# Two blocks on one core: modulation quarters in two banks with the index key behind them, and x turned chunk by chunk with the norms' roots behind the products

## The reference, cut to what matters

```python
def _hybrid_layer(x, c, w_ada, b_ada, g_norm, w_in, ...):
    mod = jax.nn.silu(c) @ w_ada + b_ada
    shift, scale, gate = jnp.split(mod, 3, axis=-1)
    h = _rms_norm(x, g_norm) * (1.0 + scale[:, None, :]) + shift[:, None, :]
    proj = h @ w_in
    qa, ka, va, za, q_idx, k_idx, w_idx, qb, kb, vb, zb = jnp.split(proj, COL_SPLITS, axis=-1)
    k_idx = _rms_norm(k_idx, k_norm_idx)
    ...
    return x + gate[:, None, :] * y

def second_block(x, positions, attn_norm_g, w_in, ...):
    h = rms_norm(x, attn_norm_g[l])        # norm 2
    proj = h @ w_in[l]
    shifted = token_shift(proj[..., :RWKV_SHIFT_DIM], rwkv_mu[l])
    ...
    x = x + y @ w_out[l]
    h = rms_norm(x, ffn_norm_g[l])         # norm 3
    gate = conv1d(h @ w_gate) + conv_b
    x = x + (silu(gate) * (h @ w_up)) @ w_down
    return rms_norm(x, final_norm_g)
```

## Time and profile before

| | |
|---|---|
| median of 3 runs | 1993.59 us |
| profiled execution, its own time | 1993.05 us |
| its span (first to last instruction) | 1991.3 us |
| mean granted TensorE clock | 0.981 |
| PE / POOL / DVE / ACT busy | 95% / 67% / 46% / 41% |
| moved by DMA | 352.6 MB, mean 177 GB/s |

### The profile page before, as it was taken

One profiled execution on the slowest core, in us unless ns is written; L12 is line 12 of the kernel. 1 busy time (PEld: TensorE's weight loads), 2 busy tenths in 40 slices (PEclk: granted clock), 3 DMA queues, 4 the chain that ended last, 5 costly groups with the idle time before them and its releaser, 6 DMA issues.

```text
span 1991.3 us, 32274 instructions
## 1 busy us (share of the span) xinstructions
PE 1892.2 (95%) x12975; PEld 1582.5 (79%) x12975; DVE 906.2 (46%) x1122; ACT 809.2 (41%) x1095; POOL 1325.3 (67%) x683
## 2 busy tenths in 40 slices
PE   5889999999989899998999999999999999999997
PEld 2668878888657798887789877888888888888886
DVE  1004647560351324565644361654455555733223
ACT  3224444444444454333422444434334343433333
POOL 2448878888239489962543496798888888844442
PEclk8899999999999999999999999999999999999999
DMA  9984545555765356543100145455555555555553
GB/s 328 363 306 164 176 168 175 189 187 190 283 223 180 112 163 212 191 147 127 46 25 4 48 167 176 162 190 189 181 181 187 190 190 180 182 196 197 194 190 127
DMA packets 174433, 352.60 MB, mean 177 GB/s; under 512 B 6735, under 2 KB 19421, under 8 KB 171773
## 3 DMA queue, kind: packets, MB, share of 16 engines
q1 hardware_dynamic: 173437, 346.94, 52.4%
q10 hardware_dynamic: 896, 4.20, 0.6%
HBM read 349.02 MB, written 2.10 MB: 176 GB/s over the span
## 4 chain that ended last, share of the span: by engine, by line
PE 59%; POOL 20%; issue 18%; DVE 2%; ACT 1%; POOLq 0%; DVEq 0%; ACTq 0%
PE bank L919 21%; POOL WL L547 19%; PE bank L921 10%; PE bank L873 6%; PE bank L874 6%; PE bank L875 6%; PE bank L1265 5%; PE bank L1185 1%; PE bank L1195 1%; PE bank L1228 1%; PE bank L395 0%; PE bank L1154 0%; POOL HX L840 0%; POOLq L546 0%; POOL arena L814 0%
## 5 line engine op out<-in xcount | busy, mean ns | idle before, releaser
L547 POOL TENSOR_TENSOR WL<-WR,WH 128x1024 fp32r<-128x1024 f32 (+2 forms) x516 | 1229.4, 2393 | 487.1 <-ACT WH L1478 485.6
L1478 ACT ACTIVATE WH<-WR 128x1024 fp32r<-128x1024 f32 (+2 forms) x560 | 577.4, 1037 | 813.3 <-PE bank L875 450.3
L919 PE MATMUL bank<-HX,WH 128*128 128x512 f32 x1840 | 649.6, 398 | 6.9 <-POOL WL L547 5.2
L921 PE MATMUL bank<-HX,WL 128*128 128x256 f32 x1840 | 515.4, 280 | 0.0
L919 PEld LDWEIGHTS bank<-HX,WH 128*128 128x128 f32 x1840 | 345.6, 188 | 92.5 <-issue 5.9
L873 PE MATMUL bank<-WH,HX 128*128 128x512 f32 (+2 forms) x864 | 339.1, 393 | 12.3 <-POOL WL L547 7.3
L921 PEld LDWEIGHTS bank<-HX,WL 128*128 128x128 f32 x1840 | 347.2, 189 | 0.0
L875 PE MATMUL bank<-WH,HX 128*128 128x512 f32 (+2 forms) x864 | 331.5, 384 | 0.0
L874 PE MATMUL bank<-WL,HX 128*128 128x512 f32 (+2 forms) x864 | 331.3, 383 | 0.0
L873 PEld LDWEIGHTS bank<-WH,HX 128*128 128x128 f32 x864 | 163.0, 189 | 50.9 <-issue 14.0
L874 PEld LDWEIGHTS bank<-WL,HX 128*128 128x128 f32 x864 | 163.2, 189 | 31.1 <-issue 1.9
(11 more groups left out here) (295 smaller groups left out, 1957.9 us busy)
## 6 DMA issues: line engine op xcount, KB each, us to landing
WR<-in_w_in SPq DMA_DIRECT2D x96, 1024.0 KB, 5.0
WR<-in_ffn_w_gate SPq DMA_DIRECT2D x44, 1024.0 KB, 5.1
WR<-in_ffn_w_up SPq DMA_DIRECT2D x44, 1024.0 KB, 5.1
WR<-in_ffn_w_down SPq DMA_DIRECT2D x44, 1024.0 KB, 5.1
arena<-in_w_ada SPq DMA_DIRECT2D x64, 512.0 KB, 9.4
WR<-in_w_out SPq DMA_DIRECT2D x32, 1024.0 KB, 5.1
WR<-in_w_ada SPq DMA_DIRECT2D x16, 1024.0 KB, 5.1
WR<-in_w_in SPq DMA_DIRECT2D x12, 768.0 KB, 4.3
```

The costliest lines, as they stand in the source:

```text
L547: eng.tensor_tensor(half(WL, n % NSLOT, *w), half(WR, n % NSLOT, *w), half(WH, nth(n) % 2, *w), ALU.subtract).then_inc(ready, 1)
L919: pe.matmul(bank[:, :].rearrange("p (h n) -> p h n", h=2), wh[:, k, o], HX[:, :, kk, :], start=kk == 0, stop=False, skip_group_check=True)
L921: last = pe.matmul(bank[:, 0:L], wl[:, k, o], HX[:, 0, kk, :], start=False, stop=kk == KT - 1, skip_group_check=True)
L1478: act.activation(half(WH, nth(n) % 2, *w), half(WR, n % NSLOT, *w), ACT.Copy).then_inc(hi_ready, 1)
```

## The change

Three things are edited.

**Start.** Even quarters of the modulation go to BANK 0 and odd ones to BANK 1, so `mod_piece` waits for `mod_ready` from the third quarter on only. A quarter has three projection pieces. The index key is one piece of 16 row tiles by 128 columns (`n_kw`) behind the last quarter. SP's order is spaced anew, and ACT puts the first `high` of a quarter ahead of the row copy. PE turns the key inside chunk j = 1 (`key_turn`), and turns back the spread key inside chunk 2 (`key_spread`); ACT's share of it (`take_key`, `take_spread`) stands between `high(n + 2)` and `high(n + 3)`.

**Norms 2 and 3.** X is turned unscaled: groups 0 to 5 inside the output chunks of the next column chunk, groups 6 and 7 inside the first chunk that uses them. They go to buffers of their own, HX2 and HX3. The products are those of unnormed x. rstd comes in behind: ACT multiplies the c chunks as it takes them; for the rest PE spreads rstd over the partitions (`row_of`, ones × diag), DVE copies that row (`row_to`) and multiplies each product by it (`by_token`): one for wag, 6 in rkv, 22 in gate and up.

**Places.** Banks of output chunks, wag and c chunks are allotted anew, as are RAWF, CV, UPS, AH, AL and the gate row.

```diff
+        n_kw = n_in + 3 * PIECES
+        n_br = n_kw + 1 - PIECES
...
-            ada_quarter(0, 4, 8)
+            ada_quarter(0, 4, 7)
             for q in range(4):
                 in_piece(q, 0)
+                ada_quarter(q, 7, 8)
+                if q < 3:
+                    ada_quarter(q + 1, 0, 2)
                 in_piece(q, 1)
                 if q < 3:
-                    ada_quarter(q + 1, 0, 3)
+                    ada_quarter(q + 1, 2, 4)
                 in_piece(q, 2)
                 if q < 3:
-                    ada_quarter(q + 1, 3, 5)
-                in_piece(q, 3)
-                if q < 3:
-                    ada_quarter(q + 1, 5, 8)
+                    ada_quarter(q + 1, 4, 7)
+            load(n_kw, w_in[:, KW_COL:KW_COL + P].rearrange("(k p) n -> p k n", p=P), P, KT)
...
                 i = n % 8
                 pe.wait_ge(ada_in[n % 4], 32 * (n // 4 + 1))
-                if i == 0 and n >= 8:
-                    pe.wait_ge(mod_ready, n // 8)
+                if i == 0 and n >= 16:
+                    pe.wait_ge(mod_ready, n // 8 - 1)
                 for g in range(4):
                     o = slice(32 * g, 32 * g + 32)
-                    last = pe.matmul(BANK[0][o, :], CA[:, 2 * i + g // 2, :], ada_w[n % 4][:, g * CH:(g + 1) * CH],
+                    last = pe.matmul(BANK[n // 8 % 2][o, :], CA[:, 2 * i + g // 2, :], ada_w[n % 4][:, g * CH:(g + 1) * CH],
                                      start=i == 0, stop=i == 7)
                 last.then_inc(ada_done, 1)
...
-                for i, (token, first, width) in enumerate(((False, 1, P), (False, 4, CH), (False, 6, CH), (True, 2, CH))):
+                for i, (token, first) in enumerate(((False, 4), (False, 6), (True, 2))):
                     if q < 3:
...
-                    if q == 3 and i == 1:
-                        pe.wait_ge(kiT_taken, 1)
+                    piece(n_in + 3 * q + i, q, token, first, CH)
+            pe.wait_ge(act_took, 2)
+            piece(n_kw, 0, False, 4, P, KT)
...
+            def key_turn(kk):
+                if kk == 2:
+                    pe.wait_ge(kiT_taken, 1)
+                    pe.wait_ge(act_took, 4)
+                    for t in range(TT):
...
+                    last.then_inc(ki_ready, 1)
+            def key_spread(kk):
...
                         for t in range(TT):
-                            last = pe.transpose(BANK[0][:, t * P:t * P + P], KIT[:, t * P:(t + 1) * P], ident[:])
...
+                    last.then_inc(kixT_ready, 1)
...
-                    if b == 0 and j == 1:
...
+            def turn_x(g, base, updated):
+                pe.wait_ge(x_updated, updated + 2 * (g // 2 + 1))
+                to_feature(X, g, 4, base)
...
+            def row_of(bank, q):
+                pe.wait_ge(xn_ready, 2 * (q + 1))
+                for t in range(TT):
+                    last = pe.matmul(BANK[bank][:, t * P:(t + 1) * P], ones, diag[:, t, :], start=True, stop=True)
+                last.then_inc(row_ready, 1)
...
+                def begin(kk):
+                    if kk in (6, 10):
+                        turn_x(2 * (c - 1) + (kk == 10), 16, 0)
+                return begin
             for c in range(4):
                 if c >= 2:
                     pe.wait_ge(x_updated, 2 * (c - 1))
-                tok_chunk(n_wo + PIECES * c, c % 2, CH, **(dict(begin=taken(8, turn_y)) if c == 0 else {}))
+                tok_chunk(n_wo + PIECES * c, c % 2, CH, begin=beside_out(c))
...
-            pe.wait_ge(xn_ready, 4)
-            turn_x = lambda g: to_feature(X, g, 4, 16, scaled=True)
-            turn_x(0)
-            turn_x(1)
...
-            wide_chunk(n_wag, 0, 3 * P, begin=taken(16, turn_x))
...
+            def last_turns(base, updated, ht):
...
+                    if kk in (4, 6):
+                        turn_x(6 + (kk == 6), base, updated)
+                    if kk % 2 == 0:
+                        pe.wait_ge(ht_ready, ht + kk // 2 + 1)
+                return begin
+            pe.wait_ge(x_updated, 6)
+            wide_chunk(n_wag, 6, 3 * P, begin=last_turns(16, 0, 16), hx=HX2)
+            row_of(1, 1)
+            pe.wait_ge(xT_taken, 2 * 24)
...
-                    pe.wait_ge(xT_taken, 2 * 24)
...
-                tok_chunk(n_c + PIECES * j, 2 + (1 + j) % 2, C_WIDTH[j])
+                tok_chunk(n_c + PIECES * j, (2, 1, 2)[j], C_WIDTH[j], hx=HX2)
...
+                    pe.wait_ge(row_ready_taken, 1)
...
+                wide_chunk(n_rkv + PIECES * j, 4 * j, CH, more=i * (2 * PIECES), hx=HX2)
...
-                        last = product(BANK[(4 + 2 * c) % 8 + t][:, :], (HH[:, kk, o], HL[:, kk, o]),
+                        last = product(BANK[(4, 6, 0, 6)[c] + t][:, :], (HH[:, kk, o], HL[:, kk, o]),
...
+                if m == 12:
+                    pe.wait_ge(x_updated, 8 + 4)
+                if m in (9, 10, 11, 12, 13, 14):
+                    turn_x(m - 9, 35, 8)
                 out2_piece(m)
...
-            pe.wait_ge(xn_ready, 6)
-            turn_x = lambda g: to_feature(X, g, 4, 35, scaled=True)
...
+                last_turns(35, 8, 28)(kk)
+                if kk == 12:
+                    row_of(7, 2)
...
+                for f in range(2):
+                    act.activation(hf[:, g % 2, f, :], BANK[4 + (base + g) % 2][:, f * L:(f + 1) * L], ACT.Copy,
+                                   scale=gains[2 * g + f]).then_inc(xT_taken, 1)
...
             for q in range(4):
+                high(n_in + 3 * q)
                 act.wait_ge(ada_done, 8 * (q + 1))
-                act.activation(mod_row, BANK[0][:, :], ACT.Copy).then_inc(row_took, 1)
-                high(n_in + 4 * q)
+                act.activation(mod_row, BANK[q % 2][:, :], ACT.Copy).then_inc(row_took, 1)
+                high(n_in + 3 * q + 1)
                 act.wait_ge(mod_ready, q + 1)
                 for k in range(4 * q, 4 * q + 4):
                     act.activation(xT[:, k, :], xT[:, k, :], ACT.Identity, bias=mod[:, k:k + 1],
...
-                    act.wait_ge(piece_done, n_in + 13)
-                    act.activation(KIT, BANK[1][:, 0:L], ACT.Copy).then_inc(kiT_taken, 1)
-                high(n_in + 4 * q + 2)
-                high(n_in + 4 * q + 3)
-            act.wait_ge(ki_ready, 1)
-            for t in range(TT):
-                act.activation(KI[:, t, :], BANK[0][:, t * P:t * P + KW], ACT.Copy).then_inc(act_took, 1)
+                high(n_in + 3 * q + 2)
...
             take_queries(0)
...
+            def take_key():
+                act.wait_ge(ki_ready, 1)
+                for t in range(TT):
...
+                act.wait_ge(ki_var, 1)
+                sqrt_of(krstd, krstd).then_inc(ki_rstd, 1)
...
+            def take_spread():
+                act.wait_ge(kixT_ready, 1)
+                act.activation(KB.rearrange("p a n -> p (a n)"), BANK[7][:, :], ACT.Copy).then_inc(kb_ready, 1)
...
                     if b or j:
                         high(n + 2, more, **relus(0))
+                        if b == 0 and j < 3:
+                            (take_key, take_spread)[j - 1]()
                         high(n + 3, more, **relus(1))
...
+                        if b + j == 0:
+                            act.wait_ge(piece_done, n_kw)
+                            for t in range(TT):
+                                act.activation(stage[:, 0, t, :], BANK[2 + t][:, :], ACT.Copy).then_inc(act_took, 1)
+                            act.wait_ge(piece_done, n_kw + 1)
+                            act.activation(KIT, BANK[4][:, 0:L], ACT.Copy).then_inc(kiT_taken, 1)
+                            high(n_br + PIECES + 1)
+                            continue
...
+                high(n + 2)
+                squares(c - 1, XN2, 0)
+                high(n + 3)
+                take_one(hf2, 2 * c - 2, 16, 16, gains2)
+                high(n + 4)
+                take_one(hf2, 2 * c - 1, 16, 16, gains2)
+                high(n + 5)
+            high(n_wag + 2)
...
                 act.dma_start(pos_i[:, t:t + 1], a["positions_2"][0, t * P:(t + 1) * P].rearrange("(p o) -> p o", o=1)) \
                    .then_inc(pos_in, 16)
+            take_one(hf2, 6, 16, 16, gains2)
+            take_one(hf2, 7, 16, 16, gains2)
+            high(n_wag + 3)
             norm_act(1)
-            take_split(hf2, 8, 16, 16, n_wag, [col("attn_norm_g_2", k) for k in range(KT)])
             act.wait_ge(ang_ready, 1)
             act.activation(ang.rearrange("p s t n -> p (s t n)"), turns.rearrange("p s t n -> p (s t n)"),
                            ACT.Sin).then_inc(trig_ready, 1)
             rest_then_next(n_wag, rest=False)
+            act.wait_ge(rstd_ready, 2)
...
                         dst = KPE[:, t, :] if which == 2 else CQ[:, 2 * which + t, c0:c1]
-                        ins = act.activation(dst, BANK[4 + 2 * ((1 + j) % 2) + t][:, b0:b1], ACT.Copy)
...
             for m in range(6, 4 * PIECES + 2):
+                if 11 <= m <= 16:
```

(38 more changed lines are left out.)

151 lines of the change are left out of this document (79 added, 72 removed).

## The result

The changed kernel takes 2001.43 us (median of 7 runs, 1999.47 to 2009.21); beside them on the same chip the kernel before took 1988.01 (7 runs). The ratio is 1.0073, with a 95% interval of 1.005 to 1.0096: 0.7% slower. The forecast was 1976. The profiled execution has a span of 1999.7 us, 8.4 more than that of before.

A forecast was written before the change was run, and what follows sets the result against it. PE, working 95% of the span, was taken to bound the kernel. Start −1.3, norm 2 +6.3 and norm 3 +12.7 made a 17.7 us gain from 1993.05, forecast as 1976, with its own range of 1970 to 1982.

The forecast's parts named there:

- Start: From the start to the head transposes: earlier columns, then a wait at the heads; a loss of 1.3 us in all.
- with both the columns come at 144.7 − 6.8 = 137.9: Start: moving key pieces behind the columns and removing DMA dips brings the last modulation columns forward by 6.8 us.
- the dips of the DMA: Start: three windows with DMA share 0.70 instead of 1.05, as PE holds modulation buffers; 1.6 us each, together 4.8.
- the 2.0 and 4.8 us: Start: 2.0 us from three key pieces no longer ahead of the last columns, 4.8 from three DMA dips.
- the wait at the heads: Start, ahead of the head transposes: PE waits 5.5 us for the key's copy, sums, spreading and scaling chain.
- Banks and places moved: Moved banks and buffer places: cost put at nothing, as the trace showed no wait on them.
- Norm 3: Last output product to gate chunk's end: 26.1 us against 38.8, a gain of 12.7; range 9 to 13.5.
- the turns: Norm 3: six turns of X moved into the output chunks, 0.4 us each, 2.4 us together.
- Norm 2: Last output product to first c product: PE waits 9 us ahead of c chunks; gain 6.3, bounds 0 and 17.2.
- Multiplications by rstd: 29 on DVE at 2.02 us, 58 us on an engine that waits: value 0, bounds 0 and 73.
- the rule of the Trainium skill: A two-SBUF-input DVE operation and an SBUF-reading GpSimd operation exclude each other; a multiplication would delay POOL its full 2.0 us.
- my rival of the pacemaker: Rival 3: POOL becomes pacemaker in rkv, gate and up; multiplications cost 73 us, total 2048; 4% chance.

The follow-up runs named there:

- e6_after_places_2048: The changed kernel with AH, AL and HX3 at multiples of 2048 bytes and HX2 at a multiple of 512: 1992.21 us.
- e10_norms_places_heads: Norms 2 and 3 with the old start, angles first, sine last, AH/AL/HX3 at 2048-byte multiples, HX2 at 512, heads scaled in one operation: 1974.75 us, ratio 0.9937.
- e15_all_mended: The changed kernel with scaling first, third modulation piece early, heads in one operation, angles first, sine last, places mended: 1967.00 us, ratio 0.990 of the kernel before.
- e4_norms_alone: The changed kernel with the start of the kernel before, leaving norms 2 and 3 and the new places: 1990.69 us, ratio 1.0036 of the kernel before.
- e9_after_heads_one_op: The changed kernel with DVE's eight multiplications scaling a chunk's heads written as one: 1996.18 us, ratio 1.0045 of the kernel before.
- e12_after_no_rstd: The changed kernel without its 29 multiplications by rstd: gate and up 498.6 us instead of 500.0, down 246.2 instead of 248.3; whole time not given.

## Why the prediction was wrong

**Start, the step of the sum that failed** (forecast +1.3, measured +9.8). The step was "with both the columns come at 144.7 − 6.8 = 137.9". They came at 144.50. I had read the dips of the DMA as time that would be given back once the banks alternated. Shown is that the period of a quarter hangs on a chain. In the changed kernel, at the second quarter:

```profile
81.12 2.00 ACT L1532 ACTIVATE WH<-WR 128x1024 fp32r<-128x1024 f32 x2 [6.47 <-DMA WR<-in_w_in]
83.03 2.06 ACT L1605 ACTIVATE arena<-arena,small 128x256 f32<-128x256 f32 x4
84.55 2.54 POOL L554 TENSOR_TENSOR WL<-WR,WH 128x1024 fp32r<-128x1024 f32 x1
84.91 2.72 DVE L1983 TENSOR_TENSOR HX<-arena,HX 128x512 fp32r<-128x512 f32 x1
```

ACT waited 6.5 us for a transfer, rounded for 2.0, and only then scaled. POOL took up the piece just rounded, and DVE's subtraction for HX beside it took 2.72 us. So the rounding ahead of the scaling cost twice: in each of the first three quarters this subtraction takes 2.7 us in the changed kernel, and 0.69 in the kernel before and wherever the scaling stood first. PE's bank was free earlier, and PE waited for the third piece and for HX instead (2.5 and 1.8 us at the second quarter). In the kernel before, what ACT rounded at this place was the small key piece, over at 77, ahead of the columns at 81.33. With rounding and loads reordered the columns were at 137.6, so a start of that length can be had; its condition was missing from the change. That 137.6 lies so near the 137.9 does not show that the 2.0 and 4.8 us it was made of are right; no run takes them apart. The second part, the wait at the heads, was forecast at 5.5 and measured at 6.49, at the place named; but that was luck: its working was wrong in two terms that made up for each other. The key's spreading took 0.87 us instead of 5.2, the heads' scaling 11.77 instead of 8.15. I had carried durations over from rows as if they belonged to the operation.

**Down projection, the largest single miss** (forecast 0, measured +9.0). "Banks and places moved" was costed at nothing, since no wait on them stood in the trace. The rate of the products changed. With AH and AL at multiples of 2048 bytes, products are 0.680 apart (three profiles of before, and those of e6_after_places_2048, e10_norms_places_heads and e15_all_mended); otherwise 0.697 to 0.700 (all eleven others). The edit of 32 bytes alone in the kernel before does it. 7.0 of the 9.0 us are that. The other 2 are a wait for DVE, which the run without the multiplications took away.

**Norm 3** (forecast −12.7, measured −8.0). No waits remain at its place, as forecast. Mis-sized were the turns. They stand in the output chunks with 5.5 us instead of 2.4: two waits of 0.5 and 1.77 us, the second for the update of X that group 3 to 5 needs (at 1221.72), and 0.54 instead of 0.4 per turn. That is 3.1 of the 4.7 that are missing; another 1.4 are the multiplications in gate and up (below). 0.2 stays open.

**Norm 2** (forecast −6.3, measured −5.4). Right in mechanism, place and size: 9 us of wait forecast, 8.91 measured, ended by POOL behind the sine. Angles first and sine last took it away. The turns cost 2.9 instead of 2.4.

**Multiplications by rstd** (value 0, bound 73). About 3.5 us. I held the rule of the Trainium skill (SBUF — State Buffer, "SBUF: two separate sides") against POOL's rows, and dismissed it since POOL's operation was lengthened by 0.5 us at most. The exclusion was there, and in the kernel before most of it fell on DVE. A multiplication of the heads that began during one of POOL's halves ended 0.1 us behind it and took up to 2.5 us; the others took 0.28. Of the eight, three waited in the kernel before (8.15 us), five in the changed one (11.77) and seven with the key's copy first (15.73), for POOL there ran with no pause in which DVE's next could slip through. One of 1024 columns took 2.90. DVE's reductions out of the banks kept their 0.68 us beside POOL. In the changed kernel POOL paid as well: each of its 19 halves over 3 us began while DVE multiplied 1024 columns (by rstd, or gate by up behind it). That agrees with the page's exclusive lock, and with its sentence that the other one fully blocks. So my rival of the pacemaker looked at the right place: POOL ended four waits of PE in the network. Its price was far off, for a half that was hit was held up by 1.0 us, with 3.4 us to spare in a chunk, and not by 2.6 for each multiplication.

**The level of rkv, gate and up** (+2.3 in rkv). Pairs are 0.3467 or 0.3533 apart; in rkv three profiles have 0.349 (e4_norms_alone, e9_after_heads_one_op, e12_after_no_rstd). For gate and up the kernel before had both in its three unchanged profiles; its medians on different occasions went from 1983.59 to 1993.51. None of the 13 profiles with HX3 had 0.3467 there. If the kernel before has the faster level in about half of its executions and the changed one never, that is some 4 to 5 us of the ratio, and could explain why the medians differ by 13.4 us and the two profiles by 8.4. Part of it may be the start, which scatters too: block 1's last input product came at 513.6 to 518.2 in the seven profiles with the old start and at 526.7 to 529.9 in the five with the new one, 12 us apart on average instead of 9.8. Neither was tested, and what sets the level is open. So is why a place of AH at a multiple of 2048 bytes matters to the matmul, and which step between 128 and 2048 is enough.

The sum of the forecast was −17.7 and of the profiles +8.4. Of the 26 us between, 8.5 are the start, 9.0 the down projection, 4.7 norm 3, 2.3 rkv, 0.9 norm 2, 0.7 attention.

## What to carry to other kernels

Read a small operation's duration as a wait: where the same form shows 0.9 us here and 5.2 there, it belongs to what ran beside it, and one large operation is cheaper than eight small ones on an engine that is locked out by its neighbour. A bound on that cost read from one engine's rows alone misses what the other pays. A gap in transfers is no reserve until the chain that frees the buffers has been followed through each engine's order, and an edit that frees one link must be checked for what stands ahead of the next. When a buffer moves, compare matmuls per window at the same granted clock, not only waits.
